# A long convolution's transforms taken by frequency halves, with the inverse's first half in between, and half of an output projection laid between a head norm's steps

## What is computed

```python
u = rms_norm(x, norm_mix_g); proj = u @ w_in
hy = short_conv(proj[..., :1536])                      # z, g1, g2: 512 channels each
spec = rfft(two-sided filter from a small MLP, per order o)
z, g1, g2 = split(hy)
for o, gate in enumerate((g1, g2)):
    conv = irfft(rfft(z, n=2 * L) * spec[:, o], n=2 * L)[:L]
    z = gate * (conv + z * skip[o])
y_hy = group_rms_norm(z, hy_norm_g, 8)
y_ml = group_rms_norm(mlstm_bidirectional(...), ml_norm_g, 4)
h = x + concat([y_hy, y_ml]) @ w_out                   # then cross-attention, MLP, second block
```

## Time and profile before

| | us |
|---|---|
| median of three runs | 2158.41 (2156.51 to 2159.41) |
| the profiled execution's own time | 2159.17 |
| its span in the trace | 2157.4 |
| TensorE busy | 2045.5 (95%), mean granted clock 0.974 |
| VectorE, ScalarE, POOL busy | 945.1, 735.6, 351.3 |
| first filter product to the last product of the projection's tile 3 | 260.10 to 445.65 |

### The profile page before, as it was taken

One profiled execution on the slowest core, in us unless ns is written; L12 is line 12 of the kernel. 1 busy time (PEld: TensorE's weight loads), 2 busy tenths in 40 slices (PEclk: granted clock), 3 DMA queues, 4 the chain that ended last, 5 costly groups with the idle time before them and its releaser, 6 DMA issues.

```text
span 2157.4 us, 26948 instructions
## 1 busy us (share of the span) xinstructions
PE 2045.5 (95%) x11390; PEld 1200.6 (56%) x11390; DVE 945.1 (44%) x1209; ACT 735.6 (34%) x1154; POOL 351.3 (16%) x358
## 2 busy tenths in 40 slices
PE   7999979699999999999999999999988799999997
PEld 5644435365766444687557444448655366444466
DVE  5654575555544332225556322323645545232224
ACT  5432221143434432124445223212454534322213
POOL 1011200021012220005003412101600015211100
PEclk9999989899999999999999999999989899999999
DMA  6211210023222223331212332223111112222321
GB/s 228 79 59 39 78 39 0 20 79 117 98 98 79 98 98 109 106 115 62 79 62 76 110 105 98 98 99 116 62 57 40 39 60 79 98 98 100 115 98 40
DMA packets 28179, 179.64 MB, mean 83 GB/s; under 512 B 2912, under 2 KB 7136, under 8 KB 7136
## 3 DMA queue, kind: packets, MB, share of 16 engines
q1 hardware_dynamic: 27264, 170.93, 22.8%
q10 hardware_dynamic: 512, 4.94, 0.6%
q0 software_dynamic: 288, 2.10, 0.3%
HBM read 175.86 MB, written 2.10 MB: 82 GB/s over the span
## 4 chain that ended last, share of the span: by engine, by line
PE 86%; DVE 8%; ACT 4%; issue 1%; DMA 0%; POOL 0%; ACTq 0%; DVEq 0%
PE psum_a L363 24%; PE psum_a L365 24%; PE psum_a L364 24%; PE psum_b L495 2%; PE psum_a L689 2%; PE psum_a L706 2%; DVE X L1684 1%; PE psum_a L617 1%; PE psum_den L615 1%; DVE RINV L1658 1%; PE psum_b L981 1%; ACT W_PARTS L1121 1%; DVE W_PARTS L1664 1%; PE psum_b L595 1%; DVE ARENA L1684 1%
## 5 line engine op out<-in xcount | busy, mean ns | idle before, releaser
L1664 DVE SCALAR_TENSOR_TENSOR W_PARTS<-W,W_PARTS 128x2048 f16<-128x2048 f32 x145 | 332.6, 2297 | 622.8 <-ACT W_PARTS L1121 622.7
L363 PE MATMUL psum_a<-U,W_PARTS 128*128 128x512 f16 (+1 forms) x1304 | 489.8, 376 | 11.5 <-DVE MIX L1792 6.0
L364 PE MATMUL psum_a<-U,W_PARTS 128*128 128x512 f16 (+1 forms) x1304 | 489.4, 375 | 0.0
L365 PE MATMUL psum_a<-U,W_PARTS 128*128 128x512 f16 (+1 forms) x1304 | 489.3, 375 | 0.0
L1121 ACT ACTIVATE W_PARTS<-W 128x2048 f16<-128x2048 f32 x145 | 276.0, 1907 | 501.5 <-PE psum_a L365 501.5
L363 PE MATMUL psum_a<-ARENA,W_PARTS 128*128 128x256 f16 (+2 forms) x956 | 295.9, 310 | 3.0 <-DVE W_PARTS L1664 3.0
L364 PE MATMUL psum_a<-ARENA,W_PARTS 128*128 128x256 f16 (+2 forms) x956 | 295.9, 309 | 0.0
L365 PE MATMUL psum_a<-ARENA,W_PARTS 128*128 128x256 f16 (+2 forms) x956 | 295.8, 309 | 0.0
L363 PEld LDWEIGHTS psum_a<-U,W_PARTS 128*128 128x128 f16 x1304 | 128.0, 98 | 162.7 <-issue 9.5
L365 PEld LDWEIGHTS psum_a<-U,W_PARTS 128*128 128x128 f16 x1304 | 128.2, 98 | 148.3 <-issue 1.7
L364 PEld LDWEIGHTS psum_a<-U,W_PARTS 128*128 128x128 f16 x1304 | 128.1, 98 | 147.3 <-issue 4.0
(11 more groups left out here) (282 smaller groups left out, 2724.4 us busy)
## 6 DMA issues: line engine op xcount, KB each, us to landing
W<-weights SPq DMA_DIRECT2D x159, 1024.0 KB, 4.9
CON<-const ACTq DMA_DIRECT2D x1, 3071.5 KB, 11.8
X<-x_in SPq DMA_DIRECT2D x2, 1024.0 KB, 7.4
U<-dft POOLq DMA_DIRECT2D x1, 1024.0 KB, 5.5
ARENA<-dft POOLq DMA_DIRECT2D x1, 1024.0 KB, 5.2
ARENA<-mem_in ACTq DMA_DIRECT2D x1, 1024.0 KB, 4.8
y_out<-U SPq DMA_DIRECT2D x2, 512.0 KB, 3.0
y_out<-U SPq DMA_DIRECT2D x4, 256.0 KB, 2.2
```

What stands on the lines that cost most here:

```text
L363: nc.tensor.matmul(out, left(0), right(0), start=first, stop=False)
L364: nc.tensor.matmul(out, left(0), right(1), start=False, stop=False)
L365: return nc.tensor.matmul(out, left(1), right(0), start=False, stop=last)
L1664: nc.vector.scalar_tensor_tensor(out=home[:, 1, :], in0=W[g % 2][:, :], scalar=W_SCALE, in1=home[:, 0, :], op0=ALU.mult, op1=ALU.subtract) ...
```

## The change

- The transforms are taken by halves of the frequencies: z's half 0, the filter's half 0, z's half 1, the filter's half 1. The product and mirror of half 0 are made as soon as its spectra are there, and the inverse's half 0 is issued before the product of half 1 is done. Four tiles of the product move from the taps' regions to SQ, ROOT and RINV.
- z of order 0 is turned first of all. The mLSTM head norm's reciprocal, scaling and low parts come on VectorE behind the butterflies of z's half 0, its head roots on TensorE behind z's half 0, ScalarE's high parts likewise.
- The filters of order 1 are made in two groups around the inverse's second half of order 0: three in ring B, five in ring A. The weight split `used(("og", 1))` is moved behind them.
- The output projection's tiles 0 to 3 take their mLSTM rows (kt 4 to 7) first, tile 0 ahead of the head sums, tiles 1 and 2 ahead of the head roots, tile 3 behind them, and then all four their long-convolution rows (kt 0 to 3). The hy head roots use ring B.

```diff
-        YC, YS = HS, HD
+        early = SQ[:, :, :].rearrange("p a b -> p (a b)").rearrange("p (a b) -> p a b", a=2)
+        YC = (early[:, 0, :], HS[:, 1, :], early[:, 1, :], HS[:, 3, :])
+        YS = (ROOT[:, :], HD[:, 1, :], RINV[:, :], HD[:, 3, :])
...
+        def filter_ring(o, tt, d):
+
+            return B if o and 2 * tt + d < 3 else A
...
+            def transform(what, o, kt, sources):
+
+                for part in range(2):
+                    for odd in range(2):
+                        bank = reuse(A, (what, o, kt, part, odd))
+                        for n in range(2):
+                            last = nc.tensor.matmul(bank[:, :], FDFT[:, part, odd, n, kt * P:(kt + 1) * P],
+                                                    sources[part][:, 2 * odd + n, :], start=n == 0, stop=n == 1)
+                        last.then_inc(A.done, 1)
+
+            def inverse_transform(o, kt):
+
+                pe.wait_ge(sem("mirrored"), 2 * o + kt + 1)
+                for ct in range(4):
+                    bank = A.bank(("y", o, ct)) if kt else reuse(A, ("y", o, ct))
+                    for odd in range(2):
+                        for part, y in ((0, HC), (1, HSN)):
+                            last = nc.tensor.matmul(bank[:, HALVES[odd]], y[:, 2 * odd + kt, ct * P:(ct + 1) * P],
+                                                    IDFT[:, part, kt, HALVES[odd]], start=kt + part + odd == 0, stop=kt + part + odd == 3)
+                    if kt:
+                        last.then_inc(A.done, 1)
+
+            turn_z(0)
             pe.wait_ge(sem("sine"), 2)
-            filters(0)
+            filters(0, range(8))
             head_sums("ml", 4, lambda h: EVEN[:, h, :], one_row)
-            turn_z(0)
-            head_roots("ml", 4, ROWS[0:64, 3, :], row_back)
-
+            pe.wait_ge(sem("fdft_landed"), 16)
 
             for o in range(2):
-                if o:
-                    filters(1)
-                    turn_z(1)
+                pe.wait_ge(B.freed_sem(("zt", o, 3)), B.freed_at(("zt", o, 3)))
+                transform("zspec", o, 0, (ZT, ZT))
                 if o == 0:
-                    pe.wait_ge(sem("fdft_landed"), 16)
+                    head_roots("ml", 4, ROWS[0:64, 3, :], row_back)
                 pe.wait_ge(sem("taps"), 8 * (o + 1))
...
+                transform("spec", o, 0, (HS, HD))
+                transform("zspec", o, 1, (ZT, ZT))
+                transform("spec", o, 1, (HS, HD))
                 if o == 0:
                     pe.wait_ge(sem("idft_landed"), 16)
-
-
-                banks = [reuse(A, ("y", o, ct)) for ct in range(4)]
-                for kt in range(2):
-                    pe.wait_ge(sem("mirrored"), 2 * o + kt + 1)
-                    for ct in range(4):
-                        for odd in range(2):
-                            for part, y in ((0, HC), (1, HSN)):
-                                last = nc.tensor.matmul(banks[ct][:, HALVES[odd]], y[:, 2 * odd + kt, ct * P:(ct + 1) * P],
-                                                        IDFT[:, part, kt, HALVES[odd]], start=kt + part + odd == 0, stop=kt + part + odd == 3)
-                        if kt == 1:
-                            last.then_inc(A.done, 1)
+                inverse_transform(o, 0)
+                if o == 0:
+                    filters(1, range(3))
+                inverse_transform(o, 1)
+                if o == 0:
+                    filters(1, range(3, 8))
+                    turn_z(1)
+
+            out_panels = []
+
+            def out_tile(j, tiles):
+                if len(out_panels) <= j // 2:
+                    w, g = panel()
+                    panel_of.setdefault("out", g)
+                    out_panels.append((w.rearrange("p l (k c) -> p l k c", k=KT), g))
+                w, g = out_panels[j // 2]
+                bank = A.bank(("out", j)) if ("out", j) in A.at else reuse(A, ("out", j))
+                for kt in tiles:
+                    pe.wait_ge(sem("hy_low" if kt < 4 else "ml_low"), kt % 4 + 1)
+                    last = product(bank[:, :], lambda l: w[:, l, kt, (j % 2) * P:(j % 2 + 1) * P], lambda l: MIX16[:, l, kt, :],
+                                   kt == 4, kt == 3)
+                    if kt == 3:
+                        last.then_inc(A.done, 1)
+                        released[g] = A.done, A.at["out", j] + 1
+
+            out_tile(0, range(4, 8))
             head_sums("hy", 4, lambda h: PR[h], lambda ct: half[:, 62 - 2 * ct:126 - 2 * ct])
-            head_roots("hy", 4, ZT[0:64, 0, :], lambda ct: gback[:, ct, :])
-            project("out", 8, MIX16, first_wait=lambda kt: pe.wait_ge(sem("hy_low" if kt < 4 else "ml_low"), kt % 4 + 1),
-                    tail="x", middle=lambda: norm_sum("mem", 0))
+            out_tile(1, range(4, 8))
+            out_tile(2, range(4, 8))
+            head_roots("hy", 4, ZT[0:64, 0, :], lambda ct: gback[:, ct, :], B)
+            out_tile(3, range(4, 8))
+            for j in range(4):
+                out_tile(j, range(4))
+            tile_list["out"] = [(("out", j), j, slice(0, T), j // 2 if j % 2 else None) for j in range(4)]
+            project("out", 8, MIX16, tail="x", middle=lambda: norm_sum("mem", 0), first=2)
 
...
+            def turned(o):
+                for tt in range(4):
+                    copy_out(B, ("zt", o, tt), ZT[:, tt, :], B.bank(("zt", o, tt))[:, :])
+
+            def even_copies(what, o, kt):
+                for part in range(2):
+                    if what == "spec":
+                        when_free(act, A, ("zspec", o, kt, part, 1))
+                    elif o:
+                        when_free(act, A, ("spec", 0, kt, part, 1))
+                    key = (what, o, kt, part, 0)
+                    copy_out(A, key, EVEN[:, 2 * kt + part, :], A.bank(key)[:, :])
+
+            turned(0)
             root_table()
             for h in range(4):
                 act.wait_ge(sem("ml_gated"), h + 1)
                 nc.scalar.activation(EVEN[:, h, :], QK[:, h, :], ACT.Square).then_inc(sem("ml_squared"), 1)
             root_rows("ml", ROWS[0:64, 2, :], P)
-            used(("og", 1))
-            for tt in range(4):
-                copy_out(B, ("zt", 0, tt), ZT[:, tt, :], B.bank(("zt", 0, tt))[:, :])
-            for h in range(4):
-                key = ("rn", "ml", h)
-                high(A.freed_sem(key), A.freed_at(key), MIX16[:, 0, 4 + h, :], QK[:, h, :], "ml_high")
-
-
             for o in range(2):
-                for tt in range(4 * o):
-                    copy_out(B, ("zt", o, tt), ZT[:, tt, :], B.bank(("zt", o, tt))[:, :])
-                for what in ("spec", "zspec"):
-                    for kt in range(2):
-                        for part in range(2):
-                            n = 2 * kt + part
-                            if what == "zspec":
-                                when_free(act, A, ("spec", o, kt, part, 1))
-                            elif o:
-                                when_free(act, A, ("zspec", 0, kt, part, 1))
-                            key = (what, o, kt, part, 0)
-                            copy_out(A, key, EVEN[:, n, :], A.bank(key)[:, :])
+                even_copies("zspec", o, 0)
+                if o == 0:
+                    for h in range(4):
+                        key = ("rn", "ml", h)
+                        high(A.freed_sem(key), A.freed_at(key), MIX16[:, 0, 4 + h, :], QK[:, h, :], "ml_high")
+                even_copies("spec", o, 0)
+                even_copies("zspec", o, 1)
+                even_copies("spec", o, 1)
+                if o == 0:
+                    used(("og", 1))
+                    turned(1)
             for ct in range(4):
                 act.wait_ge(sem("z_gated"), 5 + ct)
                 nc.scalar.activation(PR[ct], HY[:, ct, :], ACT.Square).then_inc(sem("hy_squared"), 1)
             root_rows("hy", ZT[0:64, 1, :], 64)
             for ct in range(4):
                 key = ("rn", "hy", ct)
-                high(A.freed_sem(key), A.freed_at(key), MIX16[:, 0, ct, :], HY[:, ct, :], "hy_high")
+                high(B.freed_sem(key), B.freed_at(key), MIX16[:, 0, ct, :], HY[:, ct, :], "hy_high")
 
 
...
+            def ml_norm():
+                for h in range(4):
+                    scale_rows(("rn", "ml", h), QK[:, h, :], QK[:, h, :], par("ml_norm", h))
+                for h in range(4):
+                    low("ml_high", h + 1, MIX16[:, 1, 4 + h, :], QK[:, h, :], MIX16[:, 0, 4 + h, :], "ml_low")
+
...
+            dve.wait_ge(sem("ml_gated"), 4)
+            for o in range(2):
+                butterflies("zspec", o, 0)
+                if o == 0:
+                    inverse_rows("ml", ROWS[0:64, 3, :], ROWS[0:64, 2, :])
+                    ml_norm()
+                    dve.wait_ge(sem("ml_low"), 4)
                 dve.wait_ge(sem("taps"), 8 * (o + 1))
+                butterflies("spec", o, 0)
+                multiply(o, 0)
```

(85 more changed lines are left out.)

67 lines of the change are left out of this document (20 added, 47 removed).

## The result

The changed kernel took 2135.74 us (median of four runs, 2133.56 to 2138.11) against 2158.72 for the kernel before, measured beside it: 23.0 us less, a ratio of 0.9896 with an interval of 0.9878 to 0.9913. The forecast was 2137, from 2128 to 2147.

A forecast was written before the change was run, and what follows sets the result against it. TensorE carries 86% of the chain, so only its idle and half-clock time can go: idle -17.9, clock -5.5, together -23.4, with +2.1 given back, makes -21.3 us. Forecast 2137 us, range 2128 to 2147.

The forecast's parts named there:

- The six gaps: TensorE's idle gaps from the first filter product to the projection's first four tiles: 14.5 us forecast against 32.4 before.
- the cover is 6.9 + 2.7: First convolution: inverse's first half (6.9 us) and three filter products (2.7) run beside VectorE's second product and mirror.
- The clock: Half-clock loss of TensorE in the stretch: 10.5 us forecast against 16.0 before, a gain of 5.5.
- gap 1: New 4.8 us TensorE wait ahead of the mLSTM head roots, for the reciprocal behind z's butterflies on VectorE.
- gap 6: Second convolution, behind the inverse's first half: 4.4 us left of 10.56, with no filter products as cover.
- gap 3: First convolution, ahead of the inverse's second half: the old gap of 10.56 us falls to 1.7.
- Rival (a): The short gaps each bring the clock down, costing 5 to 15 us: 2142 to 2152, chance 0.16.
- Rival (b): Kinder clock: no fall after the 1.7 us gap, first bout ends with the roots; 2128 to 2132, chance 0.11.
- (c): The inverse's first half stays behind the second product in both convolutions, not hidden: 2148, chance 0.03.
- (d): Slower than before: the low clock behind the reciprocal's gap does not end, 2235 if kept throughout; chance 0.04.
- Rival (e): No change seen: a wait behind the stretch, such as a late panel, takes back nearly all; chance 0.02.
- The panel given back: Behind the projection's four tiles, the next matrix's first panel lands late, delaying squares and memory norm sum by 2.1 us.

The follow-up runs named there:

- after_again: The changed kernel unaltered, measured and profiled a second time beside its variants: 2135.73 us, ratio 0.9899 to the kernel before.
- late_inverse: Changed kernel with one wait added, so the inverse's first half also waits for the second mirror: 2154.36 us, ratio 0.998 to the kernel before.
- squares_first: Changed kernel with ScalarE's split of the next matrix's first panel moved behind the memory norm's squares: 2129.59 us, ratio 0.9873 to the kernel before.
- old_projection: Changed kernel with output projection tiles 0 to 3 put back panel by panel behind the head roots: 2147.07 us, ratio 0.9946 to the kernel before.
- projection_alone: Kernel before with only the projection's mLSTM rows moved and head roots in ring B: 2147.59 us, ratio 0.9949 to the kernel before.
- recip_first: Changed kernel with the mLSTM head norm's reciprocal ahead of the butterflies of z's first half: 2125.29 us, ratio 0.985 to the kernel before.
- both_first: Changed kernel with both edits, reciprocal ahead of z's butterflies and panel split behind the squares: 2120.04 us, ratio 0.9827 to the kernel before.

## Why the prediction was right, point by point

- **The work stays, idle and clock are what moves.** Right. TensorE has 11390 matmul instructions before and after, and the rest without idle and clock came out at 138.3 (137.9 by the lengths) against 137.2.
- **The six gaps.** 4.8, 1.4, 1.7, 0.8, 1.4, 4.4 were forecast, 4.70, 1.41, 1.65, 0.72, 1.41, 4.42 measured. Each had been found by carrying the times of the earlier trace rows through the new lists of the engines, and each was ended by the instruction named.
- **What ended the long gap before** was misread. It was the first mirror and not the last product and mirror of a convolution. The forecast doesn't rest on that reading, since the new order was stepped through with VectorE's own durations. But the words "the cover is 6.9 + 2.7" leave out that 6 us of cover were there before, and that 5.3 of each gap went because VectorE's tail became shorter.
- **Transfers hidden, other bank ring and scratch regions free.** Right: no gap of the stretch names a DMA, the three filter products in ring B took 2.85, and the product steps that write SQ and ROOT are 0.68 long and 0.60 apart like the others.
- **The clock.** The bout behind gap 1 was put at 12.1 us of work and was 12.2. The sum of the term was 1.1 to 1.5 too high, most of it behind gap 6, where the work caught was 3.0 to 3.6, not 5.6. That it came so close is in part luck, as the second profile of the same kernel shows, where the bout behind gap 3 is missing and the one behind gap 6 is longer. The prediction's "2 to 12 us lost" for three falls doesn't follow from its rows: bouts of 3.4 to 10.2 us at half pace lose 5 to 15.
- **Rival (a)**, a fall at each short gap, is out. Behind both gaps of 1.41 and the one of 0.72 the windows show 1.00. Only the one of 1.65 brought a fall, in five of the six profiles that have it (the inverse behind it took 8.60, 10.18, 8.86, 8.57 and 8.69, and 7.17 in after_again, where 7.07 is the full clock). The prediction had full products on both sides of this gap, but three filter products on 64 rows stand right ahead of it. So the runs don't tell whether its length or this work brought the fall. The Trainium skill's rule on short idles between bank groups ("TensorE: Matmul & The Clock Gate", "A second HAM failure mode: psum-queue depth-cycling") is not borne out by this trace for gaps of 1.4 us between full products, and at 1.65 us it held in five profiles of six.
- **Rival (b)** came true in part in one execution: in after_again there is no fall after gap 3, but the bout at gap 1 outlasts the roots as before.
- **Rivals (c) and (d)** are out: the inverse's first half ran at 316.58 and 373.25, ahead of the second mirrors, and no bout in the stretch was longer than some 13.5 us. The price of (c), 11 us, was too low: late_inverse, which makes this case, came out 18.6 above the changed kernel.
- **Rival (e)** is out by the time.
- **The panel given back.** 2.1 forecast, 2.19 of waiting and 2.3 of gap measured. squares_first shows that it was the split's place in ScalarE's order that held the sum up.
- **How the gain is shared out** was mis-sized. By the sum the projection's part is -6.2 - 4.3 + 2.3 = -8. The runs show 10.7 and 11.3. Of the missing 3 us 2.0 lie behind the memory norm's sum, and in old_projection longer bouts add to it. The forecast of the whole gain was 1.7 us short (21.3 against 23.0) mainly because it had nothing for the piece behind the stretch.

The 2.0 go with the clock. From the memory norm's sum to the end it is 1707.2, 1707.2 and 1707.5 us in the kernel before, in old_projection and in late_inverse, and 1705.2, 1705.4, 1705.1 and 1705.1 in the changed kernel, its second profile, projection_alone and recip_first. The code of that piece is the same in all seven. In late_inverse the 531 matmuls of the second block that are shown above take 115.00 us, as in the kernel before, and in after_again 111.80, as in the changed kernel. (In squares_first and both_first the piece is 1702.4 and 1702.5, but there the bout behind the sum is gone.) The late_inverse kernel has the late panel and the projection's part and still shows 1707.5, so these are not it. That the clock's falls move because the work gets there at another time is likely and not shown, since no run was made that moves only that. No part of the change was made for these 2.0 us, and they are luck.

## What to carry to other kernels

Carry the time of each engine's list through the new order with the durations of the old trace; six new gaps came out to 0.1 us each, and the one that a later transfer lengthened came out to 0.2. Before a gap is put down to an instruction, look at what that engine goes on to do: here 6 us of its work were already hidden, and a run that hides none of it is no measure of the gain over the kernel before. Where a step is moved behind others on one engine, look at who waits for it elsewhere: one reciprocal behind four butterflies cost some 10 us, where the whole change brought 23. A gap of a few microseconds ahead of TensorE's work is to be priced with the half clock behind it too, which here was from under half of the gap to more than all of it (1.8 behind 4.42, some 2.4 where 4.1 of a gap went, 6.1 behind 4.70). A change of a few microseconds is to be read from its stretch and not from the total alone, since 1700 us of unchanged work moved by 2.

## What the runs showed of the hardware

- Low-clock bouts are not a fixed cost of a gap. Behind the gap of 4.70 and the 64-row head roots TensorE worked 12.2 us at 0.50. Behind 4.42 with full products it was 3.0 in one profile, and in a second profile of the same kernel the clock still averaged 0.56 over the first 5.9. Behind 1.65 it was none in after_again, 2.7 (the window's) in the first profile, and about 6 in old_projection, where the inverse behind that gap took 10.18 us instead of 7.07.
- The 64-row products ran 7.14 us at the full clock without a fall, but head roots begun at the half clock ran to their end at it: 7.19 us in the changed kernel and both times in old_projection, against 3.70 in recip_first. In the kernel before they began at the full clock, which fell 0.9 us into them (275.44 and 415.45, the windows at 0.50 from 276.30 and 416.30), and took 6.40 and 6.46.
- A piece of some 1700 us with the same code took 1707.2 to 1707.5 us in three profiles and 1705.1 to 1705.4 in four, by where in it the clock fell.
